# Dense attention as one software pipeline over its 16 heads, with whole weight-block remainders on GpSimd

## The reference

```python
def _mla(h, pos, w_in, g_q, g_kv, w_uq, w_ukv, w_o):
    lat = h @ w_in
    cq, ckv, k_rope = jnp.split(lat, [Q_LORA, Q_LORA + KV_LORA], axis=-1)   # 384, 256, 32
    cq, ckv = _rmsnorm(cq, g_q), _rmsnorm(ckv, g_kv)
    q = (cq @ w_uq).reshape(B, S, 16, 64 + 32)
    kv = (ckv @ w_ukv).reshape(B, S, 16, 64 + 64)
    # rope on the last 32 of q and on k_rope, which all heads share; q scaled by 96 ** -0.5
    s = jnp.einsum('bqhd,bkhd->bhqk', qblk, k)      # 512 x 512 per head
    p = jax.nn.softmax(s, axis=-1)
    o = jnp.einsum('bhqk,bkhd->bqhd', p, v)
    return o.reshape(B, S, 16 * 64) @ w_o
```

## Time and profile before

| | us |
|---|---|
| median of 3 runs | 1234.95 (1233.28 to 1236.65) |
| profiled execution, its own time | 1235.2 |
| span of its profile | 1233.1 |
| PE / DVE / ACT / POOL busy in the span | 1181.3 / 609.2 / 355.8 / 406.4 |
| PE busy, 615.0 to 817.3 us (dense attention) | 183.6 of 202.3 |
| granted TensorE clock, whole span | 0.992 |

### The profile page before, as it was taken

One profiled execution on the slowest core, in us unless ns is written; L12 is line 12 of the kernel. 1 busy time (PEld: TensorE's weight loads), 2 busy tenths in 40 slices (PEclk: granted clock), 3 DMA queues, 4 the chain that ended last, 5 costly groups with the idle time before them and its releaser, 6 DMA issues.

```text
span 1233.1 us, 18213 instructions
## 1 busy us (share of the span) xinstructions
PE 1181.3 (96%) x5812; PEld 980.3 (79%) x5812; DVE 609.2 (49%) x1013; ACT 355.8 (29%) x692; POOL 406.4 (33%) x423
## 2 busy tenths in 40 slices
PE   8999999999999999999889989899999999999996
PEld 7888778788888888889777767678788888888885
DVE  6666744443335433553776676744534432434332
ACT  6366622312100111110556565622222100111101
POOL 3345533333222333342342231424332311232352
PEclk9999999999999999999989999999999999999998
DMA  6311122333432333332100100113233332333421
GB/s 180 103 35 36 35 69 86 99 89 102 117 88 71 101 102 102 107 103 87 37 22 16 36 17 17 35 43 111 86 102 100 113 94 79 92 102 94 122 74 69
DMA packets 176796, 97.72 MB, mean 79 GB/s; under 512 B 8817, under 2 KB 173169, under 8 KB 176753
## 3 DMA queue, kind: packets, MB, share of 16 engines
q1 hardware_dynamic: 176752, 97.17, 27.0%
HBM read 94.01 MB, written 2.10 MB: 78 GB/s over the span
## 4 chain that ended last, share of the span: by engine, by line
PE 84%; DVE 6%; issue 4%; ACT 3%; POOL 2%; DMA 0%; ACTq 0%; DVEq 0%; POOLq 0%
PE bank L1083 26%; PE bank L1085 26%; PE bank L1084 25%; PE bank L1587 2%; PE bank L1240 1%; PE bank L1224 1%; POOL w_hi L482 1%; DVE stat L2215 1%; DVE w_lo L1669 1%; DVE bpt_lo L2220 1%; ACT s_b L1014 1%; PE bank L1158 0%; DVE w_lo L1686 0%; ACT bpt_hi L1020 0%; ACT s_a L802 0%
## 5 line engine op out<-in xcount | busy, mean ns | idle before, releaser
L1669 DVE TENSOR_TENSOR w_lo<-w_raw,w_hi 128x1024 fp32r<-128x1024 f32 (+2 forms) x142 | 191.4, 1349 | 289.1 <-POOL w_hi L482 289.1
L482 POOL TENSOR_SCALAR w_hi<-w_raw 128x1024 fp32r<-128x1024 f32 (+3 forms) x150 | 174.2, 1162 | 404.9 <-PE bank L1085 404.8
L1083 PE MATMUL bank<-x_hi,w_lo 128*128 128x512 f32 x768 | 301.7, 393 | 3.8 <-DVE gate_t L1974 2.2
L1085 PE MATMUL bank<-x_hi,w_hi 128*128 128x512 f32 x768 | 299.1, 389 | 0.0
L1084 PE MATMUL bank<-x_lo,w_hi 128*128 128x512 f32 x768 | 299.0, 389 | 0.0
L1083 PEld LDWEIGHTS bank<-x_hi,w_lo 128*128 128x128 f32 x768 | 144.2, 188 | 35.1 <-DVE gate_t L1974 2.6
L1085 PEld LDWEIGHTS bank<-x_hi,w_hi 128*128 128x128 f32 x768 | 144.2, 188 | 30.5
L1084 PEld LDWEIGHTS bank<-x_lo,w_hi 128*128 128x128 f32 x768 | 144.2, 188 | 29.0
L1083 PE MATMUL bank<-f_hi,w_lo 128*128 128x512 f32 x352 | 137.8, 391 | 1.1 <-DVE f_lo L1987 1.1
L1085 PE MATMUL bank<-f_hi,w_hi 128*128 128x512 f32 x352 | 137.1, 389 | 0.0
L1084 PE MATMUL bank<-f_lo,w_hi 128*128 128x512 f32 x352 | 137.0, 389 | 0.0
(11 more groups left out here) (229 smaller groups left out, 1923.9 us busy)
## 6 DMA issues: line engine op xcount, KB each, us to landing
w_raw<-in_ffn_w_gu SPq DMA_DIRECT2D x88, 512.0 KB, 3.8
w_raw<-in_ffn_w_down SPq DMA_DIRECT2D x32, 704.0 KB, 4.4
w_raw<-in_a_w_qkv SPq DMA_DIRECT2D x10, 512.0 KB, 4.3
w_raw<-in_a_w_o SPq DMA_DIRECT2D x8, 512.0 KB, 3.6
w_raw<-in_b_w_o SPq DMA_DIRECT2D x8, 512.0 KB, 3.7
w_raw<-in_b_w_in SPq DMA_DIRECT2D x4, 672.0 KB, 4.0
w_raw<-in_b_w_uq SPq DMA_DIRECT2D x4, 576.0 KB, 4.0
x_n<-in_x SPq DMA_DIRECT2D x4, 512.0 KB, 4.7
```

The source lines that it names most:

```text
L482: pool.tensor_scalar(split_part(w_hi, s, cols, kv), raw_part(s, cols, kv), 1.0, 1.0, ALU.mult, ALU.mult) \
L1083: pe.matmul(o, ll, rh, start=start, stop=False)
L1085: return pe.matmul(o, lh, rh, start=False, stop=stop)
L1669: dve.tensor_tensor(split_part(w_lo, s, cols, kv), raw_part(s, cols, kv), f(split_part(w_hi, s, cols, kv)), ALU.subtract) \
```

## The change

The three loops over groups of four heads go. Each engine's work in this layer is written out as one pipeline of 16 slots, one a head. In a slot TensorE does the scores of the next head, the transposes of this head and the values of the one before it, and between them the query, key and value products for the next group, across the groups' ends too. The lists `B_T`, `B_Q`, `B_PROJ_Q`, `B_PROJ_K`, `B_PROJ_V` and `B_FREED` number the units in their new order, so that each wait has its constant. All waits in the layer are against constants; in the loops they were against registers, with a register instruction ahead of each.

Of the weight blocks split in this layer, the remainder is made in one instruction on GpSimd (`b_w_rest`) in place of two on VectorE: eight blocks, among them the first two of the output projection. `w_used` is counted up at the first matmul of a later unit (`mark`) in place of a matmul of the `b_k` and transposes. Queries' evacuations count on a semaphore of their own, `q_out_ready`. Outside this layer nothing is changed.

```diff
-U_BG = 8
-U_WOB = U_B + U_BG * GROUPS
+U_WOB = U_B + 4 * GROUPS
...
+B_T = [[4, 5, 6, 7], [8, 9, 10, 11], [12, 14, 15, 16], [19, 20, 21, 22], ...
+B_PROJ_Q = [[0, 1, 2, 3], [8, 9, 10, 11], [14, 16, 18, 19], [22, 24, 26, 27]]
...
@@ gpsimd
-            def b_group(g, cols0, cols1):
-                for u in range(16):
-                    wait(pool, rsum_ready, 16 * (GROUPS + g) + u + 1)
...
-                    if u == 3:
-                        w_split_hi(C_B // 2 + 1 + g, 0, cols0)
-                    if u == 7:
-                        w_split_hi(C_B // 2 + 1 + g, 1, cols1, kv=cols0 == W_UQ)
+            def b_w_rest(g, s):
+                c2 = C_B // 2 + g
+                cols = W_COLS if g == GROUPS else (W_UQ, W_UKV)[s]
+                kv = s == 1 and g < GROUPS
+                pool.wait_ge(w_hi_ready, 2 * c2 + s + 1)
+                pool.wait_ge(w_ready, 2 * c2 + s)
+                pool.tensor_tensor(split_part(w_lo, s, cols, kv), raw_part(s, cols, kv), f(split_part(w_hi, s, cols, kv)),
+                                   ALU.subtract).then_inc(w_ready, 1)
...
@@ tensor, group g < 3, its second and fourth slot
+                    hd = HG * g + 1
+                    scores(hd + 1, 0)
+                    b_q(g + 1, 2)
+                    scores(hd + 1, 1)
+                    values(hd - 1, 0)
+                    scores(hd + 1, 2)
+                    transposes(hd, 0)
+                    transposes(hd, 1)
+                    values(hd - 1, 1)
+                    b_q(g + 1, 3)
+                    scores(hd + 1, 3, mark=True)
+                    values(hd - 1, 2)
+                    transposes(hd, 2)
+                    transposes(hd, 3)
+                    values(hd - 1, 3)
...
+                    hd = HG * g + 3
+                    values(hd - 1, 0)
+                    values(hd - 1, 1)
+                    values(hd - 1, 2)
+                    scores(hd + 1, 0)
+                    scores(hd + 1, 1)
+                    b_turn_q(g + 1, 2)
+                    transposes(hd, 0)
+                    b_k(g + 1, 1)
+                    scores(hd + 1, 2)
+                    transposes(hd, 1)
+                    transposes(hd, 2)
+                    values(hd - 1, 3)
+                    scores(hd + 1, 3)
+                    transposes(hd, 3)
+                    b_turn_q(g + 1, 3)
@@ vector, the same fourth slot
+                    maximum(hd + 1, 0)
+                    maximum(hd + 1, 1)
+                    b_q_lo(g + 1, 2)
+                    pt_lo(hd, 0)
+                    maximum(hd + 1, 2)
+                    pt_lo(hd, 1)
+                    pt_lo(hd, 2)
+                    maximum(hd + 1, 3)
+                    inv(hd + 1, 0)
+                    pt_lo(hd, 3)
+                    inv(hd + 1, 1)
+                    inv(hd + 1, 2)
+                    inv(hd + 1, 3)
+                    b_q_lo(g + 1, 3)
+                    b_k_lo(g + 1, 1)
...
```

More of the change, by code:

```diff
@@ L950, in b_q_out @@
             def b_q_out(g, t):
[L952 to L957, removed]
+                if t == 0 and g:
+                    act.wait_ge(pt_done, T_B + B_Q[g - 1][3] + 1)
+                u = B_PROJ_Q[g][t]
@@ L1080, in _, with product @@
         def _(pe):
-            def product(o, lh, ll, rh, rl, start, stop):
-                pe.matmul(o, ll, rh, start=start, stop=False)
+            def product(o, lh, ll, rh, rl, start, stop, mark=False):
+                first = pe.matmul(o, ll, rh, start=start, stop=False)
+                if mark:
+                    first.then_inc(w_used, 1)
                 pe.matmul(o, lh, rl, start=False, stop=False)
@@ new lines, in transposes @@
+            def transposes(hd, i, mark=False):
+                u = T_B + B_T[hd][i]
+                pe.wait_ge(pt_free, u - 1)
+                for qb in range(NT):
+                    if i == 0:
+                        pe.wait_ge(p_ready, 16 * GROUPS + HG * hd + qb + 1)
+                    last = pe.transpose(banks[3 + u % 2][:, qb * P:(qb + 1) * P],
+                                        s_b[:, hd % 2, qb, i * P:(i + 1) * P], ident[:])
+                    if mark and qb == 0:
+                        last.then_inc(w_used, 1)
+                last.then_inc(pt_done, 1)
@@ new lines, in values @@
+            def values(hd, i, mark=False):
+                g, n = divmod(hd, HG)
+                pe.wait_ge(pt_free, T_B + B_T[hd][i] + 1)
+                if i == 0 and n == 0:
+                    pe.wait_ge(proj_free, U_B + B_FREED[B_PROJ_V[g][1]][1])
+                if i == 0 and n % 2 == 0:
+                    pe.wait_ge(o_free, O_B + hd // 2)
+                v = (slice(None), i, n // 2, slice(HD, HD + P) if n % 2 else slice(0, P))
+                p = (slice(None), n % 2, i, slice(None))
+                last = product(banks[5][:], bv_hi[v], bv_lo[v], bpt_hi[p], bpt_lo[p],
+                               n % 2 == 0 and i == 0, n % 2 == 1 and i == NT - 1, mark)
+                if n % 2 and i == NT - 1:
+                    last.then_inc(o_done, 1)
@@ L2152, in b_rotate_q @@
             def b_rotate_q(g, half):
-                wait(dve, proj_free, U_B + U_BG * g + 2 * half + 2)
+                dve.wait_ge(q_out_ready, 4 * g + 2 * half + 2)
                 ts = slice(2 * half, 2 * half + 2)
@@ new lines, in b_w_lo @@
+            def b_w_lo(g, s, part):
+                cols = W_COLS if g == GROUPS else (W_UQ, W_UKV)[s]
+                w_half_lo(C_B // 2 + g, s, cols, part, kv=s == 1 and g < GROUPS)
+            b_q_lo(0, 0)
+            krope_lo(1)
+            b_k_lo(0, 0)
+            b_v_lo(0, 0)
+            maximum(0, 0)
+            maximum(0, 1)
+            inv(0, 0)
+            b_q_lo(0, 1)
+            maximum(0, 2)
+            b_k_lo(0, 1)
+            inv(0, 1)
+            inv(0, 2)
+            maximum(0, 3)
```

799 lines of the change are left out of this document (532 added, 267 removed).

## The result

| | before | after |
|---|---|---|
| median (lowest to highest), us | 1235.28 (1233.28 to 1236.65), 4 runs | 1202.67 (1202.33 to 1203.21), 4 runs |
| ratio, 95% interval | | 0.9738 [0.9721, 0.9755] |
| profiled execution / its span | 1235.2 / 1233.1 | 1202.8 / 1201.0 |
| PE / DVE / ACT / POOL busy | 1181.3 / 609.2 / 355.8 / 406.4 | 1167.1 / 598.1 / 346.4 / 423.7 |

The changed kernel is 32.6 us faster. The forecast was 27.9 us, and its range ended 0.8 us too early. First its windows, with the stretch from the first scores (614.8 us) to the first products of the output projection behind the last head (784.6), and a middle group. Columns as there.

The account below looks back on a forecast made before the run. TensorE was taken to bound the dense attention, losing time to pauses and a lowered clock: 1235.2 - 25.4 - 5.0 + 2.5 + 0 = 1207.3 us. Its own range was 1203.5 to 1212, for 8 in 10 1203.5 to 1220.

Parts of the forecast that it names:

- The pauses, -25.4: Dense attention: TensorE's 26 pauses go, 18.4 us idle plus 0.27 us each at the edges, 25.4 us in all.
- The clock, -5.0: Dense attention: two spells at about half the granted clock, 3.3 + 1.7 us, come back.
- Rival (a): The clock falls again behind TensorE's pause ahead of the first scores: 3.3 us more, 1210.6 us; chance 20%.
- Two waits for thin covers and what I missed, +2.5: End of the fourth slot, groups 0 to 2: two waits of at most 0.5 us for transposes' banks, plus anything missed.
- 202.3 - 30.4 = 171.9 us of work: TensorE's dense stretch less waits and clock is all work; a count by unit durations from below gave 169.
- Fewer changes between transposes and values, no register instructions, 0: TensorE: about three fewer changes a group at 0.09 us and no register instructions, 0 to -1 us; taken as 0.
- The move to GpSimd, no price: Eight weight remainders, 20.2 us on GpSimd, fit its gaps; VectorE loses 13.5 us; port sharing at most 4.2 us, taken as nothing.
- The chain of a head: Fourth score block to a head's first transposes: need 2.8 us bare, about 5.0 in the third slot against 5.9 cover; no wait.
- the waits that move: Late items on VectorE or ScalarE, or remainders ahead of normalisations, bring about 13 us back: 1220 us; chance 14%.
- all pauses replaced: TensorE's pauses are all replaced by others, time within 0.3% of the kernel before: 1235 us; chance 3%.
- slower: Each of 16 heads waits 3.0 us for its chain into the first transposes, 48 us less 30.4: 1253 us; chance 4%.
- The start, 0: Ahead of the first dense scores: reordered work shifts the time between -1 and +1 us; taken as 0.

Follow-up runs that it names:

- experiment 6: Changed kernel, with early scores waiting for the exponential of the block just ahead, as if there were one bank: 1206.54 us, ratio 0.9772.
- experiment 3: Changed kernel with the eight weight remainders back on VectorE as 16 halves, the new order kept: 1205.7 us, ratio 0.9759.
- experiment 4: Changed kernel with the second of two neighbouring transpose units put behind the next product at 17 places, 73 changes for 42: 1206.71 us, ratio 0.9764.
- experiment 1: Kernel before with its loops over groups written out on all four engines, waits against constants, order kept: 1231.95 us, ratio 0.9981.
- experiment 5: Changed kernel with each of its eight weight remainders on GpSimd made twice, one behind the other: 1202.75 us, ratio 0.9741.
- experiment 2: Kernel before, order and loops kept, with the eight weight remainders made whole on GpSimd and VectorE's halves left out: 1236.27 us, ratio 1.001.
- experiment 7: Changed kernel with the first group's keys and values ahead of its query transposes, splits moved with them: 1202.65 us, ratio 0.9731.

## Why the prediction was right in its mechanism and short in its size
**The pauses, -25.4: right.** Counted by starts they were 23.0 + 2.2 = 25.2 us. The 18.4 us of idle time had to be raised by what it hides at both edges: without that the forecast would have been 7 us worse.

**The clock, -5.0: right in size**, 4.7 us by the steps at the lower level. Rival (a) did not come: the clock is 1.00 from 620.6 to 628.2 us, and the nine runs of the changed kernel had 0.996 or 0.997 over their spans. The reason I gave against it was misread: up to the fall at 620.6 us the kernel before pauses twice behind the first scores (1.45 and 0.19 us), not three times. Nor is it shown to be the reason: experiment 6 has such pauses, and its profiled execution keeps the clock. So that the clock held is in part luck, as far as my argument goes.

**Two waits for thin covers and what I missed, +2.5: this step failed, it measured 0.** I reckoned 1.8 us of cover against 2.1 us of need at the end of the fourth slot, by giving each queued copy and subtraction its full length and 0.1 us ahead of it. Two in a row take 1.09 and 1.29 us in place of 1.4 and 1.6, and the bank was free 0.15 us early. Experiment 3 puts the halves back on VectorE, and this place still costs nothing; its late starts are in the second slot, behind the halves, where the forecast named no thin cover. So neither the wait nor the place was right.

**"202.3 - 30.4 = 171.9 us of work": mis-sized, it is 169.8.** I took all that the list of waits and the clock did not name for work. In it were 24 late starts of 0.05 to 0.3 us, 3.2 us in all, which show no idle time since the modelled length of a matmul covers them, and the new order removes all but 0.2 us of them. The other way, the pauses and the clock were 0.5 us less than I took, and 0.4 us more work now stands in the stretch. The count from below had given 169 and was the better of the two; I called the 3 us between them an agreement and went by the higher one. With the two terms the miss is 2.5 + 2.1 = 4.6 us, and 1207.3 - 4.6 = 1202.7. The lower end of the range was added up wrongly besides: with all waits gone the sum is 1204.8, and with both small gains at their bounds of 1 us it is 1202.8, not 1203.5.

**Fewer changes between transposes and values, no register instructions, 0: right**, though not for the reason given. There are 28 fewer changes (70 and 42 in the order), seven a group and not three; but one costs next to nothing, since the 0.09 us on its first matmul is given back by the transposes ahead (experiment 4). The same 0.09 us stood in the count from below, 13 times a group, and belonged there, as that count took 0.36 us for each unit of transposes and so left out the 0.08. Register instructions and branches cost 2.8 us of the stretch, inside pauses that go anyway (experiment 1).

**The move to GpSimd, no price: right**, and experiment 5 bounds it. VectorE gives up 13.5 us and is only 11.1 us less busy, since its rotations are 3.1 us dearer (below), off the path. GpSimd is 17.3 us busier where I said 20: its normalisations are shorter, 706 in place of 745 ns on average, as no halves stand beside them (696 ns in experiment 2 without the halves, 811 in experiment 3 with them). What I did not say is which of the two edits gives the time. Alone, the order gives 29.5 us (experiment 3) and the move, in the place where it was tried, nothing (experiment 2); on top of the order it gives 3 us, which are the late starts behind the halves.

**The chain of a head, the waits that move, all pauses replaced, and slower (rivals b, c and d): did not come.** No transposes wait for GpSimd. **The start, 0: right**, 0.2 us earlier.

**What is open.** What brings the clock down. In the profiled executions it fell behind a pause of 2.3 us in experiment 7 and behind one of 1.8 us in experiment 4, and it did not fall behind an idle 1.4 us in the changed kernel, nor when 1.6 us and two short pauses were added in experiment 6. The length of the pause doesn't decide it. In experiment 1 the clock fell at 614.9 us, behind pauses of 0.5 and 1.4 us. In the kernel before it stood through 0.5 and 1.75 us ahead of 615.0, fell at 620.4 us behind 1.45 us more, and again at 736.5 behind 1.0 and 0.8 us. And the mean clocks of experiments 6 and 7 differ from run to run of the same kernel. No experiment took this apart, so the 4.7 us of clock are counted, and why they came back isn't shown.

## What to carry to other kernels
Where one engine is to be full, write its order so that no two products that need the same bank stand close together, and count the work that covers each bank between one use and the next. Count an engine's work from the steps between starts, kind by kind, and against the sum of waits: what is left between the two counts is late starts that no list of waits shows, and it is to be had as well. Moving work off an engine that is not full gave nothing in the old order, where the moved work was itself waited for, and 3 us in the new one: judge such a move behind the reordering, and look where it is put. And look at the granted clock of every run, not only of the profiled one, before you say what a pause does to it.

## What the runs showed of the hardware
Rotations beside GpSimd. A multiply of VectorE with both inputs in SBUF took 0.41 us alone and 1.15 us when GpSimd had started a rounding copy of a weight block 0.18 us ahead; both end within 0.3 us of each other. In the changed kernel:

```profile
631.38 1.05 POOL L489 TENSOR_SCALAR w_hi<-w_raw 128x1024 fp32r<-128x1024 f32 x1
```
```profile
631.56 1.15 DVE L2363 TENSOR_TENSOR rope_a<-q_n,cos_n 128x256 f32<-128x256 f32 x1
...
637.87 0.41 DVE L2363 TENSOR_TENSOR rope_a<-q_n,cos_n 128x256 f32<-128x256 f32 x1
```

So the VectorE instruction was held for most of GpSimd's: it ends 0.28 us behind it, less than the 0.41 us that it takes alone. By the Trainium skill, "SBUF — State Buffer", section "SBUF: two separate sides", the engine that starts first holds the shared port pair for its whole instruction; the trace agrees in sign, here with VectorE as the one that waits, where the earlier trace rows had it the other way round. The rule was read as a possible 4.2 us and cost nothing, since VectorE had 44 us to spare in the stretch.

A change from transposes to a product is nearly free, though its first matmul looks slow: 0.36 + 0.32 us against 0.44 + 0.23 us. And the clock, as told above, in one profiled execution each: at 1.00 with 1.98 us of idle time put into the first ten microseconds of scores, and at 0.57 behind a single pause of 2.34 us.
